# Attention on ScalarE: the next step's exponential issued before the copy of the transposed probabilities, for both heads

## The chip, the cores and the metric

The kernel runs on one core of one Trainium2 chip. The metric is device time in microseconds of that core; three runs of the kernel before gave 1718.31, 1719.76 and 1721.81 us, and the median, 1719.76 us, stands for it. The profiler took one further execution.

## The reference

Two layers of a diffusion backbone over 512 latent tokens and 256 context tokens with 1024 features. Each layer is a pair of attentions side by side, whose outputs are concatenated into one output projection, and a gated feed-forward part. Layer 0 pairs latent attention (`mla`, 8 heads) with windowed attention with a sink (`swa`, 8 heads); layer 1 pairs neighbourhood attention (`na`, 8 heads) with grouped attention (`gqa`, 4 heads). All of it is float32. The part that matters here is the softmax attention of one block of 128 queries:

```python
sc = jnp.einsum('bgrqd,bgkd->bgrqk', qi, k_all).astype(jnp.float32) * scale
p = jax.nn.softmax(sc, axis=-1).astype(v_all.dtype)
return jnp.einsum('bgrqk,bgkd->bgrqd', p, v_all)
```

In `swa` the keys of a block of queries are the context and a band around the block, and one more logit (the sink) enters the sum; in `na` they are the context and a window with a bias.

## The kernel before

Each engine has its own program, written out by hand, and the engines meet at semaphores. Nothing reorders it: an engine takes its instructions in the order of the code.

**The work of a step.** An attention handles its heads in pairs (`p`), and for each pair it goes over blocks of 128 queries (`u`); a step `k` is one (`p`, `u`), and both heads of it (`x` = 0 and 1) go through together. `mla` and `swa` have 4 pairs of 6 blocks, in the order 0, 4, 1, 5, 2, 3, where blocks 4 and 5 are context queries, which have 2 tiles of 128 keys. The latent blocks have 6 tiles in `mla` and 4, 5, 5, 4 in `swa`. `na` has 4 pairs of 4 blocks of 4 tiles, `gqa` 2 pairs of 4 blocks of 6 tiles. That makes 48 steps in layer 0 and 24 in layer 1.

For a step the engines do this:

1. TensorE multiplies queries by keys, the scores (L1183 and L1190 in `mla`, L1183 in `swa`, L1164 and L1168 in `na`, L1174 in `gqa`), into banks 0 to 3.
2. VectorE copies them scaled into on-chip memory and takes the minimum of each row (`minima`, L2216, in `na` L2205 and L2216), for head 0 and head 1.
3. ScalarE takes the exponential with the row's sum (`exp`, L1721).
4. VectorE inverts the sum (L2221) and GpSimd scales the row by it (L2580).
5. TensorE transposes the probabilities, one tile of 128x128 at a time (`turns`, L1125). The first half of a head's tiles goes to bank 6, which ScalarE copies out (`left`, L1704), the second half to bank 7, which VectorE copies out (`right`, L2180). There is one bank 6 and one bank 7: the transposes of the next head, or of the next operands, wait until these copies are done.
6. TensorE multiplies the transposed probabilities by the values (`pv`, L1236, in `na` L1232).

**The order around the change.** The steps are shifted against each other. While step k's probabilities are transposed, step k+1's scores already exist. TensorE's order is scores(k+1), transposes(k, head 0), `pv`(k-1), transposes(k, head 1), then now and then the transposes of the next pair's queries and keys (`prep`: in `mla` once a pair, behind its block 4, in `swa` twice, behind its second and third block, in the last pair of `na` three times), then scores(k+2). VectorE's is minima(k+1, 0), right(k, 0), minima(k+1, 1), reciprocal(k+1, 0), right(k, 1), reciprocal(k+1, 1). ScalarE's is `attention_stages` below: `probs` is the copy `left` of a step's head, `outputs` evicts the result of a finished pair. In `mla`, behind steps 1 to 8, ScalarE also splits a piece of the next weights (`out_piece`, L1696).

The line by which TensorE waits for a copy out of bank 6 or 7 is this, in `turns`:

```python
at_least(pe, free, R0 + r)
```

Of the kernel before, what the change touches and what calls it, by code (L numbers as in the profile page):

```python
# [133 lines left out]
def run_of(first, second):  # L134

    return [(st, k) for st in (first, second) for k in range(len(st.a.steps))]


def next_pair(st, second, p):

    if p + 1 < st.a.pairs:
        return st, p + 1
    return (second, 0) if st is not second else (None, 0)
# [14 lines left out]
def build(nc, I, C, out):  # L158
# [16 lines left out]
    with ctx:  # L175
# [205 lines left out]
        def norm_growth(tiles, y, h, streams):  # L381
# [9 lines left out]
                         st=accs[0] - NT + 2 * NT, nsq=NT)),  # L391
# [1101 lines left out]
        def _(act):  # L1493
# [197 lines left out]
            def out_piece(n, piece):  # L1691
                u, cols = base("out0", "w") + n, slice(512 * piece, 512 * piece + 512)
                if piece == 0:
                    act.wait_ge(mm_done, in_done(0, MLA_KT, 3))
                    w_loaded(u)
                A(w_hi[:, u % 2, cols], w_raw[:, u % 2, cols], ACT.Copy)                    .then_inc(w_hi_done if piece == 3 else piece_hi, 1)  # L1696
# [53 lines left out]
            def attention_stages(first, second):  # L1750
                run = run_of(first, second)
                first.begin()
                for x in range(2):
                    first.exp(0, x)
                for g, (st, k) in enumerate(run):
                    p, u = st.a.steps[k]
                    for x in range(2):
                        st.probs(k, x)
                        if g + 1 < len(run):
                            ahead, m = run[g + 1]  # L1760
                            ahead.exp(m, x)
                        if x == 0 and g and u == 0:
                            back, m = run[g - 1]
                            back.outputs(back.a.steps[m][0])
                    if st.a.first and k in range(1, 9):
                        out_piece((k - 1) // 4, (k - 1) % 4)
                    nxt, q = next_pair(st, second, p)
                    for i in range(len(nxt.a.preps) if nxt else 0):
                        if st.a.prep_at[i] == u:
                            nxt.prep(q, i)  # L1770
                second.outputs(second.a.pairs - 1)
# [101 lines left out]
            sizes = [4 * 512] * 2 + [4 * 256] * 2 + [2 * 8 * MLA_D, 16 * NOPE] + [2048] * 2  # L1873
            in_projection(0, sizes)
            attention_stages(attention("mla", MLA), attention("swa", SWA))
            out_projection(0)
            norm("norm1", lambda n: next_split("norm1", "up0", n))
            feed_up(0)
            feed_down(0)
            norm("norm2", lambda n: next_split("norm2", "in1", n))  # L1880
            in_projection(1, [2048] * 10)
            attention_stages(attention("na", NA), attention("gqa", GQA))
            out_projection(1)
            norm("norm3", lambda n: next_split("norm3", "up1", n))
# [782 lines left out]
```

## Time and profile before

| | |
|---|---|
| median of three runs | 1719.76 us |
| the profiled execution | 1721.04 us, its span 1719.3 us |
| TensorE busy | 1656.8 us, 96% of the span |
| VectorE busy | 1005.9 us, 59% |
| ScalarE busy | 624.3 us, 36% |
| GpSimd busy | 259.6 us, 15% |
| attention of layer 0 | 174 to 376 us of the span |
| attention of layer 1 | 1179 to 1304 us of the span |
| ScalarE L1704, copies of transposes | x163, 67.4 us |
| ScalarE L1721, exponentials | x144, 108.5 us |

The span is the time from the first to the last instruction of the profile; about 1.7 us of the execution lie around it. The profiled execution is 1.3 us longer than the median of the three runs.

### The profile page before, as it was taken

The numbers are of one execution on the slowest core, as the hardware profiler recorded it, in microseconds if no ns is written. First come the engines' busy times: TensorE is split into PE (matmuls) and PEld (weight loads), VectorE is DVE, ScalarE is ACT, GpSimd is POOL, SyncE is SP. The second block draws the span as 40 slices with busy tenths as digits, with TensorE's granted clock in tenths as the row PEclk, the third lists the DMA queues.
The fourth block names the chain that finished last, engine by engine and source line by source line (L and its number), as shares of the span: only waits on it lengthen the run. The fifth ranks groups of instructions, "written<-read, shape, count | busy, mean of one in ns | idle before, by whom it ended". The sixth has DMA issues, their size and how long they took to land.

```text
span 1719.3 us, 26521 instructions
## 1 busy us (share of the span) xinstructions
PE 1656.8 (96%) x9828; PEld 1334.2 (78%) x9828; DVE 1005.9 (59%) x1911; ACT 624.3 (36%) x1077; POOL 259.6 (15%) x420
## 2 busy tenths in 40 slices
PE   6999899999999999999999989998999999999998
PEld 2877566668898888888878878886678888888886
DVE  3666566764747777767776487215753744443445
ACT  3414555653321212121324434225543433323343
POOL 1413233331300000000000034204420300000000
PEclk9999999999999999999999999999999999999999
DMA  8586331286513353434334454323404443332243
GB/s 317 181 275 217 88 95 30 47 92 208 185 50 98 98 147 98 137 108 126 114 105 147 132 173 149 125 81 70 120 16 135 123 122 98 95 95 66 86 135 135
DMA packets 242582, 211.34 MB, mean 123 GB/s; under 512 B 54200, under 2 KB 204600, under 8 KB 242488
## 3 DMA queue, kind: packets, MB, share of 16 engines
q1 hardware_dynamic: 236186, 199.28, 39.3%
q0 software_dynamic: 4288, 9.10, 1.4%
q10 hardware_dynamic: 2016, 1.73, 0.4%
q8 instruction: 59, 0.97, 0.2%
q14 instruction: 33, 0.27, 0.1%
HBM read 186.58 MB, written 23.48 MB: 122 GB/s over the span
## 4 chain that ended last, share of the span: by engine, by line
PE 84%; DVE 4%; ACT 3%; POOL 3%; DMA 3%; issue 2%; SPq 1%; ACTq 0%; DVEq 0%
PE ps L1360 31%; PE ps L888 9%; PE ps L889 9%; PE ps L890 9%; PE ps L1125 4%; PE ps L1236 4%; PE ps L1031 3%; PE ps L1183 3%; PE ps L1370 2%; PE ps L1174 1%; PE ps L1344 1%; PE ps L1346 1%; PE ps L1345 1%; ACT arena L1721 1%; PE ps L945 1%
## 5 line engine op out<-in xcount | busy, mean ns | idle before, releaser
L1897 DVE TENSOR_TENSOR w_lo<-w_raw,w_hi 128x2048 fp32r<-128x2048 f32 (+3 forms) x112 | 204.0, 1822 | 244.3 <-ACT w_hi L1509 243.6
L888 PE MATMUL ps<-w_hi,act_hi 128*128 128x512 f32 (+2 forms) x872 | 337.9, 388 | 3.1 <-DVE act_lo L1897 2.0
L889 PE MATMUL ps<-w_lo,act_hi 128*128 128x512 f32 (+2 forms) x872 | 333.5, 382 | 0.0
L890 PE MATMUL ps<-w_hi,act_lo 128*128 128x512 f32 (+2 forms) x872 | 333.4, 382 | 0.0
L1360 PE MATMUL ps<-act_lo,w_hi 128*128 128x512 f32 (+1 forms) x912 | 278.1, 359 | 0.0
L1360 PE MATMUL ps<-act_hi,w_hi 128*128 128x512 f32 (+1 forms) x912 | 276.4, 357 | 0.0
L1360 PE MATMUL ps<-act_hi,w_lo 128*128 128x512 f32 (+1 forms) x912 | 274.4, 355 | 0.0
L1509 ACT ACTIVATE w_hi<-w_raw 128x2048 fp32r<-128x2048 f32 (+2 forms) x106 | 166.1, 1567 | 271.9 <-PE ps L890 208.3
L888 PEld LDWEIGHTS ps<-w_hi,act_hi 128*128 128x128 f32 x872 | 164.3, 188 | 40.1 <-issue 9.9
L890 PEld LDWEIGHTS ps<-w_hi,act_lo 128*128 128x128 f32 x872 | 164.3, 188 | 30.7
L889 PEld LDWEIGHTS ps<-w_lo,act_hi 128*128 128x128 f32 x872 | 164.5, 189 | 29.2
L1360 PEld LDWEIGHTS ps<-act_hi,w_lo 128*128 128x128 f32 x912 | 151.4, 189 | 27.6
L1360 PEld LDWEIGHTS ps<-act_hi,w_hi 128*128 128x128 f32 x912 | 149.1, 188 | 28.7 <-issue 3.8
L1360 PEld LDWEIGHTS ps<-act_lo,w_hi 128*128 128x128 f32 x912 | 150.4, 188 | 24.7
L1805 ACT ACTIVATE arena<-ps,conv 128x768 f32<-128x768 f32 (+1 forms) x44 | 39.0, 885 | 309.5 <-PE ps L1360 286.3
L2580 POOL TENSOR_SCALAR arena<-arena,rinv 128x256 f32<-128x256 f32 (+3 forms) x144 | 105.1, 730 | 262.0 <-DVE rinv L2221 262.0
L1953 DVE SCALAR_TENSOR_TENSOR arena<-arena,silu 128x256 f32<-128x256 f32 x336 | 137.3, 481 | 0.9
L1125 PE MATMUL ps<-ident,arena 128*128 128x128 f32 x730 | 118.6, 288 | 12.3 <-ACT arena L1704 7.5
L1125 PEld LDWEIGHTS ps<-ident,arena 128*128 128x128 f32 x730 | 79.7, 143 | 56.2 <-issue 29.7
L1721 ACT ACTIVATE arena<-arena,nb 128x768 f32<-128x768 f32 (+5 forms) x144 | 108.5, 754 | 19.6 <-DVE nb L2216 19.0
L2294 DVE SCALAR_TENSOR_TENSOR arena<-ps,conv,arena 128x511 f32<-128x511 f32 x66 | 41.6, 658 | 124.0 <-ACT arena L1805 124.0
L1704 ACT ACTIVATE arena<-ps 128x384 f32<-128x384 f32 (+2 forms) x163 | 67.4, 413 | 118.7 <-PE ps L1125 116.3
(155 smaller groups left out, 2112.1 us busy)
## 6 DMA issues: line engine op xcount, KB each, us to landing
arena<-in_ada_w SPq DMA_DIRECT2D x44, 1024.0 KB, 8.4
w_raw<-in_ffn_up SPq DMA_DIRECT2D x88, 512.0 KB, 5.2
w_raw<-in_ffn_down SPq DMA_DIRECT2D x88, 256.0 KB, 3.0
w_raw<-in_odd_w_in SPq DMA_DIRECT2D x20, 512.0 KB, 4.5
arena<-mods SPq DMA_DIRECT2D x16, 512.0 KB, 7.3
x_after_mix<-arena SPq DMA_DIRECT2D x10, 512.0 KB, 3.0
arena<-x_after_mix SPq DMA_DIRECT2D x10, 512.0 KB, 5.2
wide_raw<-in_ada_w SPq DMA_DIRECT2D x4, 1024.0 KB, 14.0
```

Of the source, the lines that this page charges most:

```text
L888: mm(out_, s_hi, m_hi, start=start, stop=False)
L889: mm(out_, s_hi, m_lo, start=False, stop=False)
L890: return mm(out_, s_lo, m_hi, start=False, stop=stop)
L1125: last = nc.tensor.transpose(bank(b)[:, n * P:(n + 1) * P], src, ident[:, :])
L1236: last = mm(o[:, t * P:(t + 1) * P], w, pt[k % 2][x][:, c, :], start=c == 0, stop=c == len(keys) - 1)
L1360: last = mm(o, wt[:, k, :], m[:, k, rows], start=st, stop=sp_)
L1509: A(w_hi[:, s, 0:n], w_raw[:, s, 0:n], ACT.Copy).then_inc(w_hi_done, 1)
L1704: A(dst, bank(6, n * P), ACT.Copy).then_inc(left_free, 1)
L1721: A(dst, src, ACT.Exp, bias=nb[:, s, x:x + 1], scale=-1.0, accum_out=rsum[:, s, x:x + 1])\
L1897: V.tensor_sub(out_, full, hi.bitcast(fp32)).then_inc(sem_, 1)
L1953: ins = V.scalar_tensor_tensor(out=ada_sum[:, v, :], in0=w, scalar=x, in1=ada_sum[:, v, :], op0=ALU.mult, op1=ALU.add)
L2580: Q.tensor_scalar(v, v, rinv[:, k % 2, x:x + 1], 1.0, ALU.mult, ALU.mult).then_inc(p_scaled, 1)
```

## The change

In ScalarE's program the two calls of the loop over heads change places. For head x of step k, the exponential of step k+1 is now issued first, and the copy of step k's transposed probabilities second. The eviction of a finished pair's result (`outputs`) keeps its place behind both. No instruction is added or taken away, and the programs of TensorE, VectorE, GpSimd and of the DMA queues are the same, row by row.

```diff
@@ -1755,10 +1755,10 @@
                 for g, (st, k) in enumerate(run):
                     p, u = st.a.steps[k]
                     for x in range(2):
-                        st.probs(k, x)
                         if g + 1 < len(run):
                             ahead, m = run[g + 1]
                             ahead.exp(m, x)
+                        st.probs(k, x)
                         if x == 0 and g and u == 0:
                             back, m = run[g - 1]
                             back.outputs(back.a.steps[m][0])
```

ScalarE, `mla`, in the second pair, before the change: the steps of block 5 (2 tiles, a copy of 1) and block 2 (6 tiles, a copy of 3). `arena` is on-chip memory, `ps` the banks, `rsum` the row sums, `nb` the minima; L1704 is the copy and L1721 the exponential; `left_done` is signalled by the transposes and `mx_done` by the minima.

```order
L1704 ACTIVATE arena<-ps 128x128 [waits left_done,pv_done]
L1721 ACTIVATE arena,rsum<-arena,nb 128x768 [waits mx_done]
L1704 ACTIVATE arena<-ps 128x128 [waits left_done,pv_done]
L1721 ACTIVATE arena,rsum<-arena,nb 128x768 [waits mx_done]
L1704 ACTIVATE arena<-ps 128x384 [waits left_done,pv_done]
L1721 ACTIVATE arena,rsum<-arena,nb 128x768 [waits mx_done]
```

The same place, changed:

```order
L1721 ACTIVATE arena,rsum<-arena,nb 128x768 [waits mx_done]
L1704 ACTIVATE arena<-ps 128x128 [waits left_done,pv_done]
L1721 ACTIVATE arena,rsum<-arena,nb 128x768 [waits mx_done]
L1704 ACTIVATE arena<-ps 128x128 [waits left_done,pv_done]
L1721 ACTIVATE arena,rsum<-arena,nb 128x768 [waits mx_done]
L1704 ACTIVATE arena<-ps 128x384 [waits left_done,pv_done]
```

Each exponential of the following step has moved ahead of the copy with which it was paired.

ScalarE, `mla`, at the step of block 4, which has a `prep` behind it (the copy that waits for `left_done` alone), before:

```order
L1721 ACTIVATE arena,rsum<-arena,nb 128x768 [waits mx_done]
L1704 ACTIVATE arena<-ps 128x128 [waits left_done,pv_done]
L1721 ACTIVATE arena,rsum<-arena,nb 128x768 [waits mx_done]
L1704 ACTIVATE arena<-ps 128x384 [waits left_done]
L1704 ACTIVATE arena<-ps 128x384 [waits left_done,pv_done]
L1721 ACTIVATE arena,rsum<-arena,nb 128x256 [waits mx_done]
```

The same place, changed:

```order
L1721 ACTIVATE arena,rsum<-arena,nb 128x768 [waits mx_done]
L1704 ACTIVATE arena<-ps 128x128 [waits left_done,pv_done]
L1704 ACTIVATE arena<-ps 128x384 [waits left_done]
L1721 ACTIVATE arena,rsum<-arena,nb 128x256 [waits mx_done]
L1704 ACTIVATE arena<-ps 128x384 [waits left_done,pv_done]
L1721 ACTIVATE arena,rsum<-arena,nb 128x256 [waits mx_done]
```

The second head's copy now stands right ahead of the copy of the `prep`, and the exponential that stood between them ahead of both.

## Rows read from the trace of the kernel before

**Rows 1.** The page, part 1: busy time, share of the span, instructions.

```profile
PE 1656.8 (96%) x9828; PEld 1334.2 (78%) x9828; DVE 1005.9 (59%) x1911; ACT 624.3 (36%) x1077; POOL 259.6 (15%) x420
```

**Rows 2.** TensorE's waits, whole span: total us, times, longest.

```profile
PE ps L1125 <- ACT arena L1704: 7.5, 18, 1.1
```

**Rows 3.** Timeline, `mla`, pair 2, block 2: start, us, engine, line, idle before.

```profile
231.37 0.87 PE L1125 MATMUL ps<-ident,arena 128*128 128x128 f32 x6
231.47 0.96 DVE L2216 CUSTOM_DVE_ANT_0 arena<-ps,band 128x768 f32<-128x768 f32 x1 [1.01 <-PE ps L1190]
232.01 0.49 ACT L1704 ACTIVATE arena<-ps 128x384 f32<-128x384 f32 x1 [1.75 <-PE ps L1125]
232.47 0.94 ACT L1721 ACTIVATE arena<-arena,nb 128x768 f32<-128x768 f32 x1
...
233.41 0.49 ACT L1704 ACTIVATE arena<-ps 128x384 f32<-128x384 f32 x1
233.93 1.56 PE L1183 MATMUL ps<-arena 64*128 64x384 f32 x8 [0.29 <-ACT arena L1704]
```

**Rows 4.** The chain of waits, `mla`, 270 to 280 us: start, us, what.

```profile
270.87 0.81 PE ps L1125 x6
...
274.02 0.37 PE ps L1125 x2
274.39 1.46 PE ps L1236 x24
...
279.36 0.59 PE ps L1236 x8
```

**Rows 5.** Timeline, `mla`, a context step with `prep` and what follows.

```profile
248.10 0.28 ACT L1704 ACTIVATE arena<-ps 128x128 f32<-128x128 f32 x1
...
248.53 0.85 PE L1125 MATMUL ps<-ident,arena 128*128 128x128 f32 x6 [0.41 <-ACT arena L1704]
...
250.49 0.43 DVE L2216 CUSTOM_DVE_ANT_0 arena<-ps,band 128x256 f32<-128x256 f32 x1 [0.52 <-PE ps L1190]
...
251.41 0.50 ACT L1721 ACTIVATE arena<-arena,nb 128x256 f32<-128x256 f32 x1
```

**Rows 6.** Timeline, `swa`, minimum and exponential of a row of 5 tiles.

```profile
308.74 0.88 DVE L2216 CUSTOM_DVE_ANT_0 arena<-ps,band,arena 128x640 f32<-128x640 f32 x1 [0.71 <-PE ps L1183]
...
309.66 0.83 ACT L1721 ACTIVATE arena<-arena,nb 128x641 f32<-128x641 f32 x1 [0.32 <-DVE nb L2216]
```

**Rows 7.** The chain of waits, `swa`, 331 to 338.7 us.

```profile
333.22 0.70 PE ps L1125 x5
...
336.98 1.24 PE ps L1236 x20
```

**Rows 8.** Timeline, `na`: minimum, exponential, and two starts of scores, eleven steps apart.

```profile
1185.09 0.70 PE L1164 MATMUL ps<-arena 64*128 64x256 f32 x4 [0.17 <-DVE nb L2216]
...
1193.20 0.42 DVE L2205 CUSTOM_DVE_ANT_0 arena<-ps,arena 128x256 f32<-128x256 f32 x1
...
1194.20 0.72 ACT L1721 ACTIVATE arena<-arena,nb 128x512 f32<-128x512 f32 x1 [0.20 <-DVE nb L2216]
...
1223.39 0.70 PE L1164 MATMUL ps<-arena 64*128 64x256 f32 x4
```

**Rows 9.** The chain of waits, `na`.

```profile
1192.09 0.63 PE ps L1164 x4
...
1193.15 0.58 PE ps L1125 x4
1193.74 1.02 PE ps L1232 x16
```

**Rows 10.** Timeline, `gqa`: minimum of the next step, loads for this step's transposes.

```profile
1267.12 0.96 DVE L2216 CUSTOM_DVE_ANT_0 arena<-ps,band 128x768 f32<-128x768 f32 x1 [1.67 <-PE ps L1174]
1267.88 0.14 PEld L1125 LDWEIGHTS ps<-ident,arena 128*128 128x128 f32 x1
```

**Rows 11.** Busy time by window, start of `na`: span, PE, PEld, DVE, ACT, POOL, granted clock, DMA share, GB/s.

```profile
1176.00:1190.00 14.00, 8.86 (x58) 5.74 (x59) 10.18 (x37) 7.90 (x18) 8.14 (x18) 0.76 0.01 1
```

## The prediction, made before the changed kernel had run

> **What bounds the kernel now.** I read the page's first part first: TensorE is busy for 96% of the span, no other engine for more than 59% [rows 1]. So a change on ScalarE, which is busy for 36%, can move the time only by making TensorE wait more or less. Next I read what TensorE waits for. Of all its waits, those of the transposes for ScalarE's copy L1704 come to 7.5 us in 18 cases [rows 2]; there are 72 steps, with two transposes each, so in most of them the copy is done before its bank is wanted again. Then I read one step in order of time, to see what hides it.
>
> The step at 231.37 us is typical [rows 3]. TensorE starts transposes(k, 0). The minimum of step k+1 starts 0.10 us later, because the scores of that step have just ended. At 232.01 the first half of the transposes is in bank 6 and ScalarE copies it; it had been idle for 1.75 us. The exponential follows at 232.47, which is also when the minimum becomes usable: 231.47 plus 1.00. So before the change the exponential hardly waits behind the copy: the copy fills a gap in which the exponential has no data yet. TensorE meanwhile goes on with `pv`(k-1), 0.59 or 1.46 us [rows 4], behind which stand transposes(k, 1); the copy ends before them. That is the path which the change touches: transposes(k, 1) need bank 6 free.
>
> **The change, step by step.** It adds no work. It makes copy(k, x) wait for minimum(k+1, x) and for the exponential behind it. Let t be the start of transposes(k, 0). The new chain is:
>
> - minimum starts at t + 0.10 and is usable after m: 1.00 us for 6 tiles (231.47 to 232.47) [rows 3], 0.92 for 5 (308.74 to 309.66) [rows 6], about 0.51 for 2 (0.43 and 0.08 for reading the accumulator) [rows 5], 1.00 for `na`'s two parts (1193.20 to 1194.20) [rows 8]; for `swa`'s 4 tiles I put 0.80 between the 5 and the 2.
> - exponential, e: 0.94 for 6 tiles [rows 3], 0.83 for 5 [rows 6], 0.72 for 4 [rows 8], 0.50 for 2 [rows 5].
> - copy to TensorE's start, c: 0.52 for 3 tiles (233.41 to 233.93) [rows 3], 0.43 for 1 (248.10 to 248.53) [rows 5], 0.45 for 2, between them.
>
> Transposes(k, 1) are due at t + T + V, where T is transposes(k, 0): 0.81 for 6 tiles, 0.37 for 2 [rows 4], 0.70 for 5 [rows 7], 0.59 for 4 (1193.15 to 1193.74) [rows 9]; and V is `pv`(k-1): 1.46 for 6 tiles, 0.59 for 2 [rows 4], 1.24 for 5 [rows 7], 1.02 for 4 [rows 9]. The new wait is w = 0.10 + m + e + c - T - V, if that is positive.
>
> `mla`, one pair, by blocks in their order:
> - block 0 (next has 2 tiles): 0.10 + 0.51 + 0.50 + 0.52 = 1.63 against 0.81 + 1.46 = 2.27: no wait.
> - block 4 (2 tiles, next 6, V 1.46): 0.10 + 1.00 + 0.94 + 0.43 = 2.47 against 1.83: 0.64. Behind it stands the `prep`, which waits for copy(k, 1). The second exponential starts when copy(k, 0) ends, t + 2.30, the copy at t + 3.24, bank 6 is free for TensorE at t + 3.67; TensorE is there at 2.47 + 0.37 = 2.84. It waits 0.83 where it waited 0.41 [rows 5]: 0.42 more.
> - block 1 (6 tiles, next 2, V 0.59): 1.63 against 1.40: 0.23.
> - block 5: as block 4, without `prep`: 0.64.
> - block 2 (next 6, V 0.59): 2.56 against 1.40: 1.16, less the 0.29 for which the scores behind it waited anyway [rows 3]: 0.87.
> - block 3 (next 6, V 1.46): 2.56 against 2.27: 0.29.
>
> Sum 3.09 us a pair, 12.4 for four. In the first two pairs ScalarE also splits weights, so that part of these waits exists already; for that I take off 1.2 by estimate: **11.2 us** (bounds 9 and 12.4).
>
> `swa`, one pair: block 0 none (1.56 against 1.61); block 4: 2.28 against 1.39, 0.89, and 0.15 more at its `prep`; block 1: 1.63 against 1.29, 0.34; block 5: 2.28 against 1.61, 0.67; block 2: 2.14 against 1.29, 0.85; block 3: 2.07 against 1.83, of which I count 0.10, since the next step's copy is a little late before too. Sum 3.0; three such pairs, and the last, without `prep`, at 1.9 by estimate: **10.9 us**.
>
> `na`: 0.10 + 1.00 + 0.72 + 0.45 = 2.27 against 0.59 + 1.02 = 1.61: 0.66 in every step. But a step is not all work of TensorE today: from 1185.09 to 1223.39 there are 11 steps, 3.48 us each [rows 8], against 3.26 of work: scores 1.06 (1192.09 to 1193.15), transposes 0.59, `pv` 1.02, transposes 0.59 [rows 9], because GpSimd's scaling and the minima are late. These waits vanish behind the new one. A step becomes 3.92: 0.44 more, 4.8 us in 11. The other five: 0.2 at the start, three with the `prep`s of `gqa` at 0.66 plus 0.1, the last none: **7.3 us**.
>
> `gqa`: the minimum starts at 1267.12, 0.76 us before the transposes of the step at hand [rows 10], so head 0's exponential has its data sooner, and `pv`, here over full 128 columns, covers the rest. Only the first step feels it: **0.3 us**.
>
> What is gained in return: GpSimd's scaled rows come a little earlier for head 1. Nobody waits for them except in `na`, and there it is in the sum.
>
> After an attention TensorE goes straight on with the output projection, so nothing absorbs the delay. Total 11.2 + 10.9 + 7.3 + 0.3 = 29.7 us. The profiled execution took 1721.0; with the sum 1750.7. It is 1.3 us above the median, so I forecast 1749 us, 1.7% slower.
>
> A rule weighed: with one bank 6 for all left halves, the rows say that other work covers most copies, 7.5 us of waits over 163 copies [rows 2]. The Trainium skill (Perfetto Trace Analysis, section Optimizing Tensor Performance) asks that independent matmul groups rotate through PSUM banks, so that the eviction of one overlaps the next group; it gives no credit for other matmuls between them. Taken alone it would put a whole exponential, 0.5 to 0.94 us, into all 72 steps, an estimate of some 55 us and a time near 1775. The trace of before disagrees, as `pv` stands in between.
>
> **The rivals.**
>
> - *The loss is much smaller, chance 0.13.* If the minimum of head 0 could be had before the bank is filled, as in `gqa` [rows 10], the copy would be late by the exponential alone. Every w falls by about 0.5 to 0.6 us: in `mla` only blocks 4, 5 and 2 keep a little, in `na` 0.1. That gives some 5 to 14 us, 1725 to 1734. Against it: at 231.47 VectorE had been idle for 1.01 us waiting for the scores [rows 3].
> - *A larger loss through TensorE's clock, chance 0.08.* At the start of `na` TensorE is busy for 8.9 of 14 us and the granted clock of that window is 0.76 [rows 11]; its two levels are 1.2 and 2.4 GHz; with stalls in nearly every step the clock could fall to the lower one again. If each of the 12 pairs of `mla`, `swa` and `na` lost 2 us to that, it would be 24 us more, 1773. Against it: the new stalls are 1.2 us at the longest, as the longest of before, 1.1 [rows 2].
> - *Faster, chance 0.03.* If the earlier exponential brought the rows to GpSimd so much earlier that TensorE never waited for it, and the copy still landed within `pv`, then the 7.5 us [rows 2] and 0.22 us in each of 16 steps of `na` [rows 8] could go: 11 us, 1709. It decides at w = 0; w is positive in five of six blocks.
> - *Nothing measurable, chance 0.02*, 1720: were the minima ready when the copy is asked for, the order would not matter. 232.47 against 232.01 says they are not [rows 3].
>
> **How the numbers follow.** The forecast holds 0.74; its own range is 1740 to 1758: the waits could be 30% smaller, since a delayed step also lets VectorE catch up, or a third larger if the `prep`s add up. The range for 8 in 10 takes in the top of the smaller loss and part of the clock's: 1733 to 1761. Slower by over 0.2% (3.4 us, about what a measurement of this kernel can tell from no change) is 0.95, the same 0.02, faster 0.03.
>
> **What would show it.** TensorE's waits for L1704 at L1125 should rise from 7.5 to some 40 us or more and from 18 cases to 60 or more, none far above 1.2 us. The cadence of `na` should be 3.9 us a step, a late pair of `mla` 3 us longer. In each step the copy should start just when an exponential ends, with ScalarE idle before the exponential for the minimum. The granted clock should stay at full speed, and all outside the attentions keep its length. I am wrong if the copy, waiting behind the exponential, still ends before `pv`, or if the clock falls.

## The result, and the profile after

The changed kernel takes 1749.08 us in the median of four runs (1747.56 to 1750.18), the kernel before beside it 1720.78: the ratio is 1.0166, with a 95% interval of 1.0154 to 1.0178. By the ratio that is a loss of 28.6 us, with 26.5 to 30.6 by the interval (the two medians lie 28.3 us apart); forecast were 1749 and a loss of 29.7 us.

The page, first part, and TensorE's waits over the whole span, of the changed kernel:

```profile
PE 1653.2 (95%) x9828; PEld 1331.8 (76%) x9828; DVE 1003.6 (57%) x1911; ACT 620.8 (36%) x1077; POOL 260.7 (15%) x420
```

```profile
PE ps L1125 <- ACT arena L1704: 43.9, 72, 1.3
```

Every engine does what it did before: the numbers of instructions are the same, and the busy times stand within 4 us of where they stood [rows 1]. The span is longer by 26.6 us (1745.9 against 1719.3), and the one kind of wait that has grown is the predicted one: transposes waiting for the copy out of bank 6, 43.9 us in 72 cases after 7.5 in 18 [rows 2]. It has grown by 36.4 us, more than the span: some 5 us of TensorE's other waits have gone (of the transposes for GpSimd, for VectorE's copy and for a transfer, and of the scores for ScalarE's copy), and TensorE is busy for 3.6 us less.

The timeline of the changed kernel at the same step as [rows 3], block 2 of the second pair of `mla`. Columns are start, us, engine, line, what, and the idle time ahead with what ended it:

```profile
231.81 0.87 PE L1125 MATMUL ps<-ident,arena 128*128 128x128 f32 x6
231.91 0.96 DVE L2216 CUSTOM_DVE_ANT_0 arena<-ps,band 128x768 f32<-128x768 f32 x1 [1.82 <-PE ps L1190]
...
232.61 0.66 PE L1236 MATMUL ps<-arena 128*64 128x128 f32 x8
...
232.91 0.93 ACT L1721 ACTIVATE arena<-arena,nb 128x768 f32<-128x768 f32 x1 [2.86 <-DVE nb L2216]
...
233.85 0.47 ACT L1704 ACTIVATE arena<-ps 128x384 f32<-128x384 f32 x1
...
234.46 0.85 PE L1125 MATMUL ps<-ident,arena 128*128 128x128 f32 x6 [1.19 <-ACT arena L1704]
```

Read it from the top. Transposes of head 0 start at 231.81, the minimum 0.10 us later. In [rows 3] ScalarE copied bank 6 0.64 us after the transposes had begun; here it sits idle until 232.91, 1.10 us after, because the exponential at the head of its queue has no minimum yet. The exponential takes until 233.85, and only then comes the copy, although its data have been there for well over a microsecond. TensorE has finished the short `pv` and stands still for 1.19 us. It resumes 2.65 us after the start of head 0's transposes; the chain in the prediction gave 2.56.

Landmarks split the loss by attention. They are starts of scores on TensorE, from the timeline: the first of pair 2 of `mla`, the first and the last of `swa`, the second and the fourth of `na`, and the second of `gqa`. Before:

```profile
204.81 1.56 PE L1183 MATMUL ps<-arena 64*128 64x384 f32 x8 [0.42 <-ACT arena L1704]
...
291.41 1.13 PE L1183 MATMUL ps<-arena 64*128 64x256 f32 x8 [0.29 <-ACT arena L1704]
...
372.95 1.13 PE L1183 MATMUL ps<-arena 64*128 64x256 f32 x8
...
1180.51 1.23 PE L1164 MATMUL ps<-arena 64*128 64x256 f32 x4 [4.69 <-DVE nb L2216]
...
1188.47 0.70 PE L1164 MATMUL ps<-arena 64*128 64x256 f32 x4
...
1242.50 1.88 PE L1174 MATMUL ps<-arena 128*128 128x384 f32 x5
```

The changed kernel, with one row more, ten steps behind the fourth scores of `na`:

```profile
203.74 1.56 PE L1183 MATMUL ps<-arena 64*128 64x384 f32 x8
...
298.57 1.13 PE L1183 MATMUL ps<-arena 64*128 64x256 f32 x8
...
390.50 1.13 PE L1183 MATMUL ps<-arena 64*128 64x256 f32 x8
...
1199.40 1.22 PE L1164 MATMUL ps<-arena 64*128 64x256 f32 x4 [4.68 <-DVE nb L2216]
...
1209.64 0.70 PE L1164 MATMUL ps<-arena 64*128 64x256 f32 x4
...
1249.11 0.70 PE L1164 MATMUL ps<-arena 64*128 64x256 f32 x4
...
1270.33 1.88 PE L1174 MATMUL ps<-arena 128*128 128x384 f32 x5
```

| stretch | before, us | after, us | loss |
|---|---|---|---|
| `mla`, pairs 2 to 4 | 86.60 | 94.83 | 8.2 |
| `swa`, first to last scores | 81.54 | 91.93 | 10.4 |
| `na`, from its second scores to `gqa`'s second | 61.99 | 70.93 | 8.9 |

Two small pieces lie behind these landmarks: 0.5 us in the last `swa` step of block 2 (from its next scores to the output projection 3.8 us after 3.3), and 0.3 behind `gqa`'s second scores. Together these are 28.4 us, against 26.6 by the two spans. The rest is not the same in the two traces either: `mla` starts 1.1 us earlier in the changed kernel, its first pair takes 30.3 us in both, the way from the output projection behind `swa` to `na`'s second scores is 0.8 us longer, and the end behind `gqa`'s last scores 1.6 us shorter. Those stretches differ by as much between traces of kernels that have the same order there. The stretches of `mla` and `swa` in the table don't: the three pairs of `mla` take 86.6 us in each of three traces with the old order there, and `swa` takes 81.5 to 81.6 us in five; with the full change it is 94.8 and 91.9 us in three traces each.

### The profile page after: what moved, and what is told of

Its sections match the earlier page's. It is cut to its first block, busy times and chain, and to the rows that moved or that the text cites. A ratio compares the mean times of both kernels' runs of the same rounds, so it can differ in the third digit from the quotient of the medians.

```text
span 1745.9 us, 26521 instructions
## 1 busy us (share of the span) xinstructions
PE 1653.2 (95%) x9828; PEld 1331.8 (76%) x9828; DVE 1003.6 (57%) x1911; ACT 620.8 (36%) x1077; POOL 260.7 (15%) x420
## 4 chain that ended last, share of the span: by engine, by line
PE 80%; DVE 5%; issue 5%; ACT 4%; DMA 2%; POOL 2%; SPq 1%; ACTq 0%; DVEq 0%
PE ps L1360 30%; PE ps L888 9%; PE ps L889 9%; PE ps L890 9%; PE ps L1125 4%; PE ps L1031 3%; PE ps L1183 3%; PE ps L1236 2%; PE ps L1370 2%; DVE arena L2216 1%; PE ps L1174 1%; ACT arena L1721 1%; ACT arena L1704 1%; PE ps L1346 1%; PE ps L1344 1%
## 5 line engine op out<-in xcount | busy, mean ns | idle before, releaser
L1721 ACT ACTIVATE arena<-arena,nb 128x768 f32<-128x768 f32 (+5 forms) x144 | 109.2, 758 | 145.4 <-DVE nb L2216 143.2
L1125 PE MATMUL ps<-ident,arena 128*128 128x128 f32 x730 | 115.7, 285 | 44.6 <-ACT arena L1704 43.9
L1125 PEld LDWEIGHTS ps<-ident,arena 128*128 128x128 f32 x730 | 79.9, 143 | 89.0 <-issue 73.5
L2180 DVE COPY arena<-ps 128x256 f32<-128x256 f32 (+2 forms) x161 | 71.9, 446 | 84.6 <-PE ps L1125 84.3
```

The lines of the kernel that those rows point to most:

```text
L1125: last = nc.tensor.transpose(bank(b)[:, n * P:(n + 1) * P], src, ident[:, :])
L1721: A(dst, src, ACT.Exp, bias=nb[:, s, x:x + 1], scale=-1.0, accum_out=rsum[:, s, x:x + 1])\
L2180: V.tensor_copy(dst, bank(7, n * P)).then_inc(right_free, 1)
```

## The experiments

The theory is the chain of the prediction: head 0's copy ends late, because the wait for the minimum and the exponential stand ahead of it, and TensorE waits wherever `pv` is too short to cover that. The rivals were that the order as such costs an even share in every step or for each head, that the wait for the minimum is what costs, and that TensorE's clock falls. All kernels are the one before with another condition for the new order (`first_exp`; the dots stand for it), where nothing else is said; their losses are the ratio to the kernel before, less one, times 1720.

```diff
                     for x in range(2):
-                        st.probs(k, x)
+                        first_exp = ...
+                        if not first_exp:
+                            st.probs(k, x)
                         if g + 1 < len(run):
                             ahead, m = run[g + 1]
                             ahead.exp(m, x)
+                        if first_exp:
+                            st.probs(k, x)
```

**One head at a time.** Head 0 alone:

```diff
+                        first_exp = x == 0
```

> Only head 0's exponential stands ahead of head 0's copy; head 1 keeps the old order. If the loss is TensorE waiting for the copy out of bank 6 before head 1's transposes, all of it is here: head 0 decides, and the same chain (0.10 + m + e + c against T + V) gives at least the 28 us of the full change. Laid out step by step it is even more, some 33 us or 1754 us, because in the steps of 4 and 5 tiles head 1's exponential, which now starts before the minimum's neighbour is copied, no longer shares the wait. Rival: each of the two moves costs half, 14 us, 1735 us.

Measured: 1752.68 us, ratio 1.0181 (1.0167 to 1.0195), a loss of 31 us. TensorE's waits of this kernel:

```profile
PE ps L1125 <- ACT arena L1704: 45.4, 77, 1.6
```

Head 0 alone carries the whole loss, and the waits are those of the full change. That it costs even more than the full change is what the medians say (31 against 28.6 us), but the two intervals overlap. The traces say it too: the pairs 2 to 4 of `mla` take 96.0 us here and 94.8 with the full change, `swa` takes 93.7 and 91.9, in stretches that otherwise repeat to 0.1 us. So head 1's exponential, moved along with head 0's, gives back some 3 us there.

Head 1 alone:

```diff
+                        first_exp = x == 1
```

> Only head 1's exponential stands ahead of head 1's copy. Behind head 1's transposes come the scores of the step after next, 0.6 to 2.6 us of TensorE's work that need no bank 6, so the copy has that cover wherever no operand transposes (prep) stand behind; laid out step by step it is 8 to 10 us, 1729 to 1731 us, most of it at the preps and in layer 0. Rival (half each): 14 us, 1735 us. If head 1 alone costs as much as both, the theory of bank 6 at head 0 is wrong.

Measured: 1727.74 us, 1.0046 (1.0032 to 1.0060), a loss of 8 us, and TensorE waits for the copy 20.1 us in 24 cases. The moves don't share the loss by halves (14 us each, outside both intervals), and their losses don't add up either: 31 and 8 against 29. Behind head 1's transposes TensorE has the next scores to do. In the trace of this kernel `swa` is 5.5 us longer than before and the three pairs of `mla` 1.8 us.

**The two parts of the delay.** The old order, but with the wait for the minimum put in front of the copy:

```diff
+                def minimum(k, x):
+                    act.wait_ge(mx_done, S0 + 2 * k + x + 1)
...
                     for x in range(2):
-                        st.probs(k, x)
                         if g + 1 < len(run):
                             ahead, m = run[g + 1]
+                            ahead.minimum(m, x)
+                        st.probs(k, x)
+                        if g + 1 < len(run):
                             ahead.exp(m, x)
```

> The old order (copy, then exponential), but the copy of each head first waits for the next step's minimum of the same head, as the exponential would. This splits the delay into its two parts: the wait for the minimum is there, the exponential's own 0.5 to 0.94 us is not. By the chain, 0.10 + m + c against T + V leaves something only where a short pv stands between: 5 to 8 us, 1726 to 1728 us. Rival: if waiting for VectorE's minimum is what costs, as the idle ScalarE of the trace suggests at first sight (143 us of waits for the minimum), nearly all of the 28 us is here, 1745 us or more.

Measured: 1724.30 us, 1.0021 (1.0011 to 1.0030), a loss of 3.6 us, less than the 5 to 8 that were expected and far from the rival's 25. ScalarE's waits, the copies for the minimum, and TensorE's:

```profile
ACT arena L1704 <- DVE nb L2221: 93.4, 68, 3.2
```

```profile
PE ps L1125 <- ACT arena L1704: 11.8, 24, 1.1
```

ScalarE waits 93 us for minima at its copies, and TensorE's waits for the copy rise by 4.3 us only. The idle time of an engine that isn't the bottleneck is not its cost here. Here is the same step as above in this kernel:

```profile
231.84 0.87 PE L1125 MATMUL ps<-ident,arena 128*128 128x128 f32 x6
...
232.95 0.49 ACT L1704 ACTIVATE arena<-ps 128x384 f32<-128x384 f32 x1 [2.19 <-DVE nb L2221]
...
233.58 0.85 PE L1125 MATMUL ps<-ident,arena 128*128 128x128 f32 x6 [0.28 <-ACT arena L1704]
```

The copy starts 1.11 us after the transposes, which is where the exponential started in the changed kernel, and TensorE waits 0.28 us in place of 1.19. The 0.91 us between them are the exponential, which took 0.93 there.

The other way round, the changed order with a short exponential in `mla`. This kernel leaves the row beyond the first 128 columns as it is and takes no minimum as bias, so its `mla` is not softmax:

```diff
+                    if a.name == "mla":
+                        A(dst[:, 0:P], src[:, 0:P], ACT.Exp, scale=-0.01, accum_out=rsum[:, s, x:x + 1])\
+                            .then_inc(exp_done, 1)
+                        return
```

> The changed order, but in mla the exponential covers one tile of 128 columns instead of 2 or 6 (and leaves the rest of the row as it is, without the minimum as bias), so the arithmetic of mla is not softmax any more; the waits are the same. e falls from 0.94 and 0.50 to about 0.39 us by the slope between the two. If e is a term of the delay, the loss in mla falls by about 9 us and the total from 28 to 19-20 us, 1740 us. Rival: if the wait for the minimum or the mere order costs, the time stays at 1748 us.

Measured: 1740.79 us, 1.0117 (1.0102 to 1.0132), a loss of 20.1 us, 8 less than the full change. The pairs 2 to 4 of `mla` take 87.4 us (200.44 to 287.80):

```profile
200.44 1.56 PE L1183 MATMUL ps<-arena 64*128 64x384 f32 x8
...
287.80 1.13 PE L1183 MATMUL ps<-arena 64*128 64x256 f32 x8
```

Of the 8.2 us that the full change costs there, 7.5 are gone. In the second pair's block 2, the step shown above, it reads like this (the exponential's line is L1722 in this kernel):

```profile
226.44 0.88 PE L1125 MATMUL ps<-ident,arena 128*128 128x128 f32 x6
...
227.54 0.31 ACT L1722 ACTIVATE arena<-arena 128x128 f32<-128x128 f32 x1 [2.90 <-DVE nb L2220]
...
227.85 0.47 ACT L1704 ACTIVATE arena<-ps 128x384 f32<-128x384 f32 x1
...
228.47 0.84 PE L1125 MATMUL ps<-ident,arena 128*128 128x128 f32 x6 [0.56 <-ACT arena L1704]
```

The exponential starts 1.10 us behind the transposes, as in the changed kernel, takes 0.31 us in place of 0.93, and TensorE resumes 2.03 us behind them in place of 2.65: the 0.62 us that the exponential is shorter come back whole. So its length is a term of the delay, and in `mla` the one that decides. What the old order would take with the short exponential wasn't run; since TensorE is busy for 83.6 of the 86.6 us before, it could be at most 3.0 us less than 86.6.

**Where the loss lies.** Only block 2 of `mla` and `swa`, the steps for which the chain gives the dearest wait:

```diff
+                        first_exp = st.a.full and u == 4
```

> The full change, but only in the steps of block 2 of mla and swa, 8 of 72 steps, where the exponential of a full row meets the short pv of a context block. By the chain these are the dearest steps, 0.8 to 1.2 us each: 7.6 us, 1728 us. Rival: the loss is spread evenly over all steps, 8/72 of 28 us, 3 us, 1724 us.

Measured: 1726.91 us, 1.0035 (1.0022 to 1.0047), a loss of 6.0 us (3.8 to 8.1): 8 of 72 steps carry a fifth of the loss. An even share, 3 us, lies below the interval. The three last pairs of `mla` are 2.6 us longer in the trace, 0.87 us for each of these steps, as the chain had it; the steps of `swa` cost 0.8 us each (0.85 by the chain) and the last one, with the output projection behind it, 0.5.

Only `gqa`, for which the chain gives nothing:

```diff
+                        first_exp = st.a.name == "gqa"
```

> The change in gqa alone. There the minimum starts 0.76 us before the transposes and pv takes 2.7 us, so the copy lands under pv though it stands behind the exponential: 0.3 us, no difference that can be measured, 1721 us. Rival (even spread over steps): 8/72 of 28 us, 3 us.

Measured: 1720.69 us, 1.0004 (0.9995 to 1.0013): no difference. An even share would be 1.0018, outside the interval.

`mla` alone and `na` alone:

```diff
+                        first_exp = st.a.name == "mla"
```

> The change in mla alone, 24 of 72 steps. My sum has 11.2 us for it; the trace of the changed kernel has 8.2 us in its pairs 2 to 4 (from the first scores of pair 2 to the first of swa, 94.8 against 86.6) and in pair 1 something between 0 and 1.6, by how the clock rises. So 8.5 to 10 us, 1729 to 1731 us. If it were 11 or more, the losses would not add up.

```diff
+                        first_exp = st.a.name == "na"
```

> The change in na alone, 16 of 72 steps. Waits laid out: 7 us, 1728 us, if they are all. With a longer stretch at the lower clock at the start: 8.5 to 9 us, 1729.5 us. If the losses of the attentions add up, this and the measured 28 leave 19 to 20 us for layer 0.

Measured: `mla` 1729.73 us, 1.0057 (1.0043 to 1.0071), 9.8 us; `na` 1728.62 us, 1.0049 (1.0037 to 1.0061), 8.4 us. With `swa`'s 10.4 us of the table, the 0.5 behind its last scores and 0.3 of `gqa`, which are read from the trace (`swa` was not run alone), the sum is 29.4 us, against 28.6 measured for all together. Within the intervals, some 2 us either way for each run, the losses add up by attention; the traces have the same 94.8 us for `mla`'s three pairs whether `swa` and `na` are changed or not.

**The clock.** The full change, but not in the first pair of `na`:

```diff
+                        first_exp = not (st.a.name == "na" and p == 0)
```

> The full change except in the first pair of na, 4 of 72 steps, where TensorE has just come from an idle stretch with the clock at its lower level. The laid-out waits of these four steps are worth 1.6 us: 1747.5 us. If the new stalls there also keep the clock low for longer, as the trace of the changed kernel shows (granted clock 0.69 in 1204 to 1209 against 1.00 in 1185 to 1190 before), some 1.5 us more come back: 1746 us, and the granted clock is at 1.00 five us after the first scores of na.

Measured: 1744.24 us, 1.0142 (1.0128 to 1.0156), 24.4 us, some 4 less than the full change. Only part of it is in the place that was edited: in the traces the `na` stretch is 2.0 us shorter than in the changed kernel, and the first pair of `mla`, which has the same order in both, by another 1.1. The windows of the granted clock (span, PE, PEld, DVE, ACT, POOL, clock, DMA share, GB/s) from `na`'s second scores on, changed kernel:

```profile
1199.00:1204.00 5.00, 3.39 (x14) 2.20 (x15) 2.93 (x14) 2.27 (x8) 3.62 (x8) 0.50 0.00 0
1204.00:1209.00 5.00, 4.59 (x32) 3.03 (x30) 2.56 (x12) 2.12 (x6) 3.61 (x8) 0.69 0.00 0
1209.00:1214.00 5.00, 4.27 (x40) 3.19 (x42) 2.99 (x16) 3.16 (x9) 2.08 (x3) 1.00 0.57 76
```

Before:

```profile
1180.00:1185.00 5.00, 4.21 (x16) 2.49 (x16) 2.93 (x14) 2.75 (x8) 3.62 (x8) 0.50 0.00 0
1185.00:1190.00 5.00, 4.65 (x42) 3.25 (x43) 3.73 (x19) 3.10 (x8) 4.52 (x10) 1.00 0.01 3
```

And without the change in `na`'s first pair:

```profile
1196.00:1201.00 5.00, 4.26 (x18) 2.53 (x18) 2.93 (x15) 2.69 (x9) 3.61 (x8) 0.50 0.00 0
1201.00:1206.00 5.00, 5.00 (x34) 3.51 (x36) 2.79 (x13) 2.15 (x6) 3.95 (x9) 0.66 0.03 4
```

After the idle stretch ahead of `na` TensorE runs at the lower level, 1.2 GHz (0.50), and the time at which it rises to 2.4 differs. The expectation that it rises early once the stalls are gone was not met: here it is 0.66 in the second window, with TensorE busy throughout. The two steps between the second and the fourth scores of `na` (1180.51 to 1188.47 before, 1199.40 to 1209.64 after) took, with the old order there, 7.96 or 7.97 us in four traces (the kernel before, `gqa` alone, block 2 alone and the selection below) and 9.4 to 9.5 in two (this kernel and `mla` alone); with only head 1's new order 7.96; with the copy waiting for the minimum 9.50; with head 0's new order 10.24 in all four that have it (the changed kernel, head 0 alone, the short exponential, `na` alone). The mean granted clock over these two steps was 0.72 to 0.75 in the five short ones, 0.57 in the three of 9.4 to 9.5, and 0.58 to 0.62 in the four of 10.24. So a late rise occurs without head 0's stalls and costs these two steps 1.4 to 1.5 us. Whether the stalls bring it about, four of four against three of eight, twelve traces don't settle.

The clock also falls later on, which the trace of the changed kernel doesn't show. These are windows of the kernel with `na` alone changed, where `na` ends and `gqa` begins:

```profile
1240.00:1245.00 5.00, 3.32 (x34) 2.16 (x30) 3.08 (x13) 2.55 (x7) 1.38 (x2) 1.00 0.01 3
1245.00:1250.00 5.00, 4.90 (x14) 2.80 (x14) 0.96 (x2) 0.97 (x3) 0.00 (x0) 0.66 0.00 0
```

And of the kernel before, outside the attentions:

```profile
1350.00:1355.00 5.00, 2.62 (x22) 2.42 (x22) 4.21 (x3) 0.69 (x2) 4.83 (x3) 1.00 0.93 265
1355.00:1360.00 5.00, 5.00 (x32) 5.00 (x31) 3.71 (x4) 1.12 (x2) 0.10 (x1) 0.66 1.02 258
```

In the first pair of windows, behind a stretch in which TensorE was busy for 3.32 of 5 us and waited for 0.64 us at the longest, part of the next window ran at the lower level, and the step from `gqa`'s first scores to its second took 6.38 us where it takes 4.72 before and in the changed kernel. It is the same in the traces of head 0 alone and of the short exponential (6.40 us each), but not in those of the full change and of this kernel, which have the same stalls there. Where head 0 keeps the old order in the last pair of `na`, one trace of seven has such a fall, that of block 2 alone, behind a wait of 1.54 us for a transfer. So a fall of the clock can cost 1.7 us at this place, in some executions and not in others; three of five against one of seven is no proof that the stalls bring it about. In `mla` behind the first pair and in `swa`, where two thirds of the loss lie, the granted clock is at 0.97 or more in every window of 5 us of all twelve traces.

**Only where it should be free.** Head 1 of blocks 5 and 3 of `mla` and head 0 of `gqa`'s first block:

```diff
+                        first_exp = (st.a.name, u, x) in (("mla", 5, 1), ("mla", 3, 1), ("gqa", 0, 0))
```

> The new order only where the laid-out steps say that it costs nothing or gains: head 1 of blocks 5 and 3 of mla, where long scores stand behind the transposes and no operands, and head 0 of the first block of gqa; 10 of 144 places. Worked out: 0.6 us faster, below what a measurement can tell, 1720 us. Rival: any exponential ahead of its copy costs, some 0.2 us a place, 2 us.

Measured: 1720.19 us, 1.0000 (0.9991 to 1.0009). The rival's 2 us (1.0012) lie outside. So the selection that the chain offers as free costs nothing and gains nothing that can be measured, and none of the versions that were tried beats the kernel before.

## Why the prediction was right

**The bound.** That ScalarE's order can only move the time through TensorE's waits was right: the busy times are unchanged, and the wait of L1125 for L1704 rose from 7.5 to 43.9 us.

**The chain.** In the step that was laid out, TensorE resumed 2.65 us after the start of head 0's transposes, against 2.56 worked out; from the copy's start to TensorE's it is 0.61 us (233.85 to 234.46) where 0.52 had been taken, and that is all of the difference. A step in the middle of `na` waits 0.64 us where 0.66 had been worked out. The two heads apart, the wait for the minimum alone and the short exponential each came out on the side of the chain.

**The terms.** `mla` was 11.2 us and measured 9.8 (7.4 to 12.2) alone; the trace has 8.2 in three pairs, where the sum without the deduction had 9.3: 2.9 in each of the late pairs against 3.09, and 2.4 in the second, in which ScalarE splits weights, so that the deduction, an estimate, was of about the right size. `swa` was 10.9 and is 10.4 in the table and 10.9 with the piece behind its last scores. `na` was 7.3 and is 8.9 in the trace and 8.4 (6.4 to 10.5) alone; a step takes 3.95 us (1209.64 to 1249.11, ten steps) against 3.92 worked out. The excess of 1.6 is at the start of `na`: the two steps took 2.3 us longer (10.24 against 7.96), of which 1.4 to 1.5 is what a late rise of the clock costs in the old order too. `gqa` was 0.3 and is 0.3. The misses cancel in part: 29.7 worked out, 28.6 measured. That the total is off by 1.1 us only is partly luck. The late rise at the start of `na` was not in the sum, and the stretches outside the attentions, which were to keep their length, moved by 1.1, 0.8 and 1.6 us, not all in one direction, between the two traces.

**The rivals.** The smaller loss would have needed the minimum before the bank is filled; the minimum starts 0.10 us behind the transposes in `mla`, as before. The clock stays at full speed in the middle of `mla` and `swa` in spite of the stalls. At the start of `na` it may hold for 1.4 to 1.5 us of the 24 that this rival was priced at, and in three other kernels for 1.7 us more at the end of `na`. What the prediction held against it, that no new stall is longer than 1.2 us, was no safe ground: there it fell behind stalls of 0.6 us. The gain would have needed the copy under `pv`, which the chain gives only for `gqa` and for block 0 of `mla` and `swa`.

**The rule on banks.** The whole exponential in every step, some 55 us, did not come. The Trainium skill (Perfetto Trace Analysis, section Optimizing Tensor Performance) lets the eviction of one bank overlap the next group in another bank; in this case's traces other work of TensorE between two uses of the same bank does as well, as far as it reaches: 43.9 us of waits in 72 cases, and none in front of head 1's transposes in `gqa`, where `pv` takes 2.8 us.

## What to carry to other kernels

On a queue that is taken in order, put first what another engine waits for soonest, here the copy that frees a bank, and what waits longest for its own input last. An instruction that isn't ready blocks a ready one behind it, and the price is its wait plus its length, less what the bottleneck engine has to do in between; working that out for each kind of step from one trace gave a loss of 29.7 us where 28.6 were measured. Idle time on the engine that is reordered (143 us behind the new exponentials by ScalarE's waits, 93 in the experiment that cost 3.6) is no measure of it.

ScalarE's waits in the changed kernel, for that last number:

```profile
ACT arena L1721 <- DVE nb L2216: 143.2, 85, 3.7
```

## What was not expected of the hardware

The moment at which TensorE's clock rises after an idle stretch differs between kernels whose program around it is the same: at the start of `na` the same two steps in the same order took 7.96 us in four traces and 9.4 to 9.5 in two, and the first pair of `mla` took 30.3 us in the profile of before (174.52 to 204.81) and 28.7 in that of the kernel changed in `gqa` alone, where nothing in front differs. For a change of a few us, one profile's stretch behind an idle time isn't evidence.

The clock can also fall in the middle of work that stalls only for short times: at the end of `na` it fell behind waits of 0.56 to 0.64 us in the kernel with `na` alone changed, and the same program in the same place kept the full clock in the changed kernel. In three traces it cost the first step of `gqa` 1.7 us.
